# A two-layer hybrid decoder step on one core: another opening, the root table loaded earlier, the output stored in four pieces

## The chip, the core and the metric

The kernel runs on one core of a Trainium2 chip. The core has TensorE (PE; its weight loads, PEld, overlap its products), VectorE (DVE), ScalarE (ACT), GpSimd (POOL) and the queue of SyncE (SP); transfers are issued from SP and POOL and run on 16 shared DMA engines. Time is the device time of one execution in microseconds (us); lower is better. Everything is float32 unless said otherwise.

## What is computed

One inference step of two layers over 256 prompt tokens and 8 sequences of 4 new tokens each, T = 288 columns in all, held as 8 tiles of 128 features. Per layer:

```
xn = rms_norm(x, norm_w)            # x * rsqrt(mean(x*x) + eps) * w
p  = xn @ w_in                      # 35 tiles of 128 output columns
A  = sparse attention over a paged cache (indexer, top-k) * silu(gate)
C  = dilated window attention, 3 groups              * silu(gate)
B  = SSD recurrence (conv, scan, gated rms_norm over groups of 192)
x  = x + concat(A, C, B) @ w_out    # 8 tiles
```

After the second layer `y = rms_norm(x, final_norm_w)` is stored, beside updated caches and states.

## The kernel before, in words

The work is written out by hand, one instruction stream per engine, with a semaphore for every hand-over. Nothing is planned by a scheduler: each engine does its list in order.

**The norm.** For N = 0 (start), 1 (between the layers) and 2 (the end), ACT squares the 8 tiles of x (`square`, L656, into the two buffers `squares`, which lie in tile `cacc`). The sum over the features is a product with a matrix of ones on PE into bank 2. Then ACT takes the square root (`root`, L661) and DVE the reciprocal, which gives `rstd` (L1512). For N = 1 and 2, the first square goes to `tmp`, DVE adds squares 1 to 5 onto it (L2136), and PE sums only three tiles: `tmp` (`sum_added`) and squares 6 and 7 (`sum_squares`). For N = 0, PE sums all eight squares, one product each, before anything else it does, and square k waits until PE has used square k - 2.

**The start.** SP issues the two halves of x (576 KB each), then the parameters `prm` (51 KB), weight tile 0 (512 KB), the page table, weight tiles 1 and 2, constants, and more. DVE multiplies each tile of x by the norm weight (`weighted`, L1517) into `xn`. PE then does `proj(0)`, `proj(1)`, `proj(2)`: 8 products each of a 128x128 weight tile with 128x288 columns. Their results are multiplied by `rstd` afterwards. From `proj(3)` on (`LATE_ROOT`), DVE has multiplied `xn` itself by `rstd` (L1754). When `proj(i)` is complete, SP loads weight tile i + 4, and SP and POOL load the first eight of the `kv` buffers, one or two per projection.

**The page stage.** After `proj(7)` come 16 page pairs, each of whose 16 products read two `kv` buffers that hold records of 8 cache pages (`in_kk`). A ring of 8 buffers is refilled as PE uses them; every second pair is followed by a projection.

**The rest of a layer.** Projections alternate with the indexer's top-k search, the recurrence, window attention and value pages. In it is the norm over groups of 192 features of the SSD result (three tiles of 128): group norm sums `gn0` in bank 2 (tile 0 and the first half of tile 1) and `gn2` in bank 7 (the second half of tile 1 and tile 2), L1426 to L1431, each a product with all or 64 rows of `ones`. At the end `output` (8 tiles) is added into x by DVE (L2130).

**The end.** The final norm's 8 tiles (L2143) are stored by SP in two pieces of 4 tiles (576 KB, L497), each when its tiles are ready.

In the listing, `mm` is one product (two PE records and two weight loads, since float32 takes two passes), `tt_` and `ts_` are DVE operations, and `S[...]` are semaphores.

## Time and profile before

| | us |
|---|---|
| median of 3 runs | 614.76 (609.92, 614.76, 616.73) |
| the profiled execution | 617.67 |
| its span, first to last instruction | 615.9 |
| PE busy / PEld busy | 593.1 / 418.7 |
| DVE / POOL / ACT busy | 357.6 / 276.1 / 169.7 |
| transferred | 198.37 MB, mean 322 GB/s |

The profile is of one execution. A timeline row gives the start and the length of a group of like instructions; "[0.46 <-ACT cacc L656]" says that the engine had been idle for 0.46 us and that ACT's write to `cacc` ended it. A matmul's length contains its latency, so how fast PE goes is read from the distance between starts, best from those of its weight loads. The granted clock is 1.00 at 2.4 GHz and 0.50 at 1.2 GHz.

### The profile page before, as it was taken

The numbers are of one execution on the slowest core, as the hardware profiler recorded it, in microseconds if no ns is written. First come the engines' busy times: TensorE is split into PE (matmuls) and PEld (weight loads), VectorE is DVE, ScalarE is ACT, GpSimd is POOL, SyncE is SP. The second block draws the span as 40 slices with busy tenths as digits, with TensorE's granted clock in tenths as the row PEclk, the third lists the DMA queues.
The fourth block names the chain that finished last, engine by engine and source line by source line (L and its number), as shares of the span: only waits on it lengthen the run. The fifth ranks groups of instructions, "written<-read, shape, count | busy, mean of one in ns | idle before, by whom it ended". The sixth has DMA issues, their size and how long they took to land.

```text
span 615.9 us, 13773 instructions
## 1 busy us (share of the span) xinstructions
PE 593.1 (96%) x4850; PEld 418.7 (68%) x4850; DVE 357.6 (58%) x1068; ACT 169.7 (28%) x429; POOL 276.1 (45%) x476
## 2 busy tenths in 40 slices
PE   5999999999999999999999999999999999999993
PEld 3776655677777766667777665557777786667772
DVE  3674655667657934843348563747776794484224
ACT  4013532223221503441111252323321250354011
POOL 0415642477721594444210275327774159544420
PEclk9999999998889989999999999999998998999998
DMA  8798999999997899999954699999999879979996
GB/s 321 253 328 297 368 367 386 406 377 363 357 378 233 244 341 295 299 314 407 352 179 136 212 368 368 373 414 391 383 356 383 299 246 348 291 225 305 363 326 230
DMA packets 80821, 198.37 MB, mean 322 GB/s; under 512 B 12049, under 2 KB 44978, under 8 KB 80242
## 3 DMA queue, kind: packets, MB, share of 16 engines
q0 software_dynamic: 28768, 102.22, 47.0%
q1 hardware_dynamic: 51986, 95.28, 44.2%
q8 instruction: 39, 0.64, 0.4%
q14 instruction: 28, 0.23, 0.1%
HBM read 189.30 MB, written 52.00 MB: 392 GB/s over the span
## 4 chain that ended last, share of the span: by engine, by line
PE 85%; DMA 9%; issue 2%; SPq 1%; DVE 1%; POOL 1%; ACT 1%; POOLq 0%; ACTq 0%; DVEq 0%
PE bank L898 82%; DMA kv<-in_kk 7%; PE bank L948 3%; DMA kv<-in_vv 1%; SPq L423 1%; DMA x<-in_x 1%; POOL kv L423 1%; DVE xn L2143 1%; DVE rstd L1512 0%; POOL xwb L547 0%; ACT cacc L656 0%; ACT L656 0%; SPq L419 0%; POOLq L419 0%; POOLq L423 0%
## 5 line engine op out<-in xcount | busy, mean ns | idle before, releaser
L898 PE MATMUL bank<-xn,w 128*128 128x288 f32 x1120 | 297.6, 421 | 0.0
L898 PEld LDWEIGHTS bank<-xn,w 128*128 128x128 f32 x1120 | 210.5, 194 | 68.7 <-issue 12.5
L423 POOL DMA_DIRECT2D kv<-in_kk x128 | 69.0, 539 | 121.7 <-issue 68.1
L423 POOL DMA_DIRECT2D kv<-in_vv x128 | 68.9, 541 | 53.5 <-PE bank L898 41.9
L689 ACT ACTIVATE pt<-bank 128x288 f32<-128x288 f32 x48 | 19.7, 411 | 231.7 <-PE bank L898 231.6
L898 PE MATMUL bank<-pt,kv 128*128 128x288 f32 x256 | 62.4, 406 | 0.0
L898 PEld LDWEIGHTS bank<-pt,kv 128*128 128x128 f32 x256 | 48.5, 190 | 13.4
L1587 DVE TENSOR_SCALAR_CACHE_REDUCE hit<-sc,tb 128x516 bf16<-128x516 f32 x62 | 46.5, 750 | 2.2
L898 PE MATMUL bank<-kv,pt 128*32 128x256 f32 x512 | 33.8, 385 | 2.5 <-DMA kv<-in_vv 2.5
L524 POOL DMA_DIRECT2D out_keep<-in_buf x48 | 24.5, 510 | 25.4 <-PE bank L898 23.6
L898 PE MATMUL bank<-kv,qz 128*32 128x256 f32 x512 | 34.3, 385 | 0.0
L2130 DVE TENSOR_TENSOR x<-x,bank 128x288 f32<-128x288 f32 x16 | 7.3, 454 | 45.4 <-PE bank L898 45.3
L1560 DVE COPY tails<-cin 128x3 f32<-128x3 f32 x14 | 5.9, 424 | 42.3 <-ACT cin L687 40.1
L413 POOL DMA_DIRECT2D kv<-in_dil x16 | 9.0, 561 | 44.5 <-PE bank L898 44.5
L1598 DVE TENSOR_SCALAR tb<-bank 128x1 int32<-128x1 f32 x62 | 9.6, 154 | 32.2 <-PE bank L898 31.6
L898 PE MATMUL bank<-kv,shared 128*32 128x128 f32 x768 | 25.8, 291 | 0.0
L898 PE MATMUL bank<-pt 64*128 64x128 f32 (+3 forms) x168 | 25.8, 332 | 0.0
L898 PEld LDWEIGHTS bank<-pt 64*128 64x128 f32 (+2 forms) x168 | 17.7, 183 | 11.0 <-issue 10.3
L898 PEld LDWEIGHTS bank<-kv,pt 128*32 128x32 f32 x512 | 13.6, 109 | 16.5 <-issue 7.6
L1566 DVE SCALAR_TENSOR_TENSOR cacc<-cin,prm,cacc 128x312 f32<-128x312 f32 x42 | 22.8, 544 | 1.5
L898 PEld LDWEIGHTS bank<-kv,shared 128*32 128x32 f32 x768 | 22.1, 116 | 0.6 <-issue 0.5
L656 ACT ACTIVATE cacc<-x 128x288 f32<-128x288 f32 x22 | 9.6, 442 | 46.2 <-DVE x L2130 42.4
(251 smaller groups left out, 818.6 us busy)
## 6 DMA issues: line engine op xcount, KB each, us to landing
w<-in_w SPq DMA_DIRECT2D x70, 512.0 KB, 7.3
out_keep<-in_buf POOLq DMA_DIRECT2D x16, 1984.0 KB, 14.3
kv<-in_kk SPq DMA_DIRECT2D x128, 160.0 KB, 8.1
kv<-in_kk POOLq DMA_DIRECT2D x128, 160.0 KB, 5.8
kv<-in_vv SPq DMA_DIRECT2D x128, 128.0 KB, 4.2
kv<-in_vv POOLq DMA_DIRECT2D x128, 128.0 KB, 4.3
kv<-in_dil SPq DMA_DIRECT2D x16, 576.0 KB, 9.7
kv<-in_dil POOLq DMA_DIRECT2D x16, 576.0 KB, 8.1
```

The source lines that it names most:

```text
L413: engine.dma_start(kv[:, s, 0:9 * P], a["dil"][layer, item]).then_inc(S[f"kv_in{s}"], 16)
L423: engine.dma_start(kv[:, s, r * rec:(r + 1) * rec], a["kk" if what == "page" else "vv"][bass.ds(page + layer * N_POOL, 1)].rearrange("o p ...
L524: pool.dma_start(dst[:, cut:].rearrange("o (r k) -> (o r) k", r=16), src[:, cut:].rearrange("o (r k) -> (o r) k", r=16)).then_inc(S["copie ...
L656: act.activation(tmp[:, :] if N and k == 0 else squares[:, k % 2, 0:T], x[:, k, :], ACT.Square).then_inc(S["sq_ready"], 1)
L689: act.activation(ptile(i), src[:, 0:T], fn).then_inc(use, 1)
L898: return pe.matmul(out, lhsT, rhs, start=start, stop=stop, skip_group_check=True, **k)
L948: return pe.transpose(out, in_, ident(n))
L1566: stt(out=o, in0=cin[:, n % 2, j:j + COUT], scalar=prmc(L, "cw", 4 * n + j), in1=o, op0=ALU.mult, op1=ALU.add).then_inc(S["cin_used"] if j ...
L1587: ts_(hit[:, :], sc[:, :], old.bitcast(F32), 0.0, ALU.is_ge, ALU.add, accum_out=cnt[:, 0:1]).then_inc(S["cnt_ready"], 1)
L1598: ts_(tb[:, 2:3], src[:, 0:1], float(TOPK_S), float(bit), ALU.is_lt, ALU.mult).then_inc(drained(f"count{n}"), 1)
L2130: tt_(x[:, m, :], x[:, m, :], src[:, 0:T], ALU.add).then_inc(drained(f"out{m}"), 1)
L2143: dve.scalar_tensor_tensor(out=xn[:, k, :], in0=x[:, k, :], scalar=fnw[:, k:k + 1], in1=rstd[:, :], op0=ALU.mult, op1=ALU.mult).then_inc(S ...
```

## The change

The opening's sums take the form that the other two norms have: the first square goes to `tmp`, DVE adds five squares onto it between its multiplications, and PE has three products of sums left, which now stand behind `proj(0)`. Ahead of `proj(0)`, PE does twelve products of `ones` with itself (`WARM`) into bank 7, whose result nobody reads. SP issues `prm` first, then the first half of x, weight tile 0, and the second half of x. ACT takes the root of one column of `eps` (`root_table`) ahead of the squares of each norm, so that the table load goes there. The two half-row products of the group norm come behind both full ones. y is stored in four pieces of 2 tiles (288 KB).

```diff
--- before.py
+++ after.py
@@ -52,6 +52,7 @@
 WSLOTS = 4
 DT_ROW, WI_ROW = 0, 32
 PSLOTS = 32
+WARM = 12
 SLOTS = {QI: 0, KI: 4, QA: 12, XBC: 5, QC: 14, KC: 17, KA: 20, VA: 22, VC: 24, GA: 27, GC: 29, ZZ: 0}
 
 
@@ -199,7 +200,7 @@
 
 
 PER = {
-    "rstd_ready": 1, "sq_ready": 8, "sq_added": 5, "sq_used": 7, ...
+    "rstd_ready": 1, "sq_ready": 8, "sq_added": 5, ...
     "qs_ready": 1, "relu_used": 1, "prelu_used": 8, "cnt_ready": NCOUNT + 1, "cin_used": 7, "tanhed": 7, "conved": 7,
     "qz_ready": 1, "qcz_zero": 1, "so_sel": 1, "qcz_ready": 6, "qcbd_ready": 6, "mask_ready": 1, "sexp_in": 1, "sexp": 1, "px_ready": 1,
     "pexp_in": 2, "pexp": 2, "pprob": 2, "dexp_in": 2, "dexp": 2, "dprob": 2,
@@ -226,6 +227,7 @@
         ones = sb("ones", [P, P])
         eps = sb("eps", [P, 1])
         fnw = sb("fnw", [P, KT])
+        rooted = sb("rooted", [P, 1])
         ptab = sb("ptab", [1, NPTAB], I32)
 
         x = sb("x", [P, KT, T])
@@ -444,10 +446,10 @@
                 sync.dma_start(w[:, n % WSLOTS, :, :].rearrange("p k n -> p (k n)"),
                                a["w"][n // NTILE, n % NTILE]).then_inc(S[f"w_in{n % WSLOTS}"], 16)
 
-            for n in range(2):
-                sync.dma_start(x[:, 4 * n:4 * n + 4, :], a["x"][:, 4 * n:4 * n + 4, :]).then_inc(S[f"x_in{n}"], 16)
             sync.dma_start(prm[:, :, :], a["prm"]).then_inc(S["prm_in"], 16)
+            sync.dma_start(x[:, 0:4, :], a["x"][:, 0:4, :]).then_inc(S["x_in0"], 16)
             load_w(0, 0)
+            sync.dma_start(x[:, 4:8, :], a["x"][:, 4:8, :]).then_inc(S["x_in1"], 16)
             sync.dma_start(ptab[:, :], a["ptab"]).then_inc(S["ptab_in"], 16)
             load_w(0, 1)
             load_w(0, 2)
@@ -492,10 +494,10 @@
                     consumed(*RING[lo:hi])
                     next_w(28 + i)
                 consumed(*RING[80:])
-            for n in range(2):
-                sync.wait_ge(S["y_normed"], 4 * n + 4)
-                sync.dma_start(a["y"][:, 4 * n:4 * n + 4, :], xn[:, 4 * n:4 * n + 4, :]).then_inc(S["y_out"], 16)
-            sync.wait_ge(S["y_out"], 32)
+            for n in range(4):
+                sync.wait_ge(S["y_normed"], 2 * n + 2)
+                sync.dma_start(a["y"][:, 2 * n:2 * n + 2, :], xn[:, 2 * n:2 * n + 2, :]).then_inc(S["y_out"], 16)
+            sync.wait_ge(S["y_out"], 64)
 
 
         @block.gpsimd
@@ -649,17 +651,20 @@
                     act.wait_ge(S[f"x_in{k // 4}"], 16)
                 else:
                     act.wait_ge(drained(f"out{k}"), nth(N - 1, f"out{k}"))
-                if N == 0 and k >= 2:
-                    act.wait_ge(S["sq_used"], k - 1)
-                if N and k >= 3:
-                    act.wait_ge(S["sq_added"], nth(N - 1, "sq_added", k - 2))
-                act.activation(tmp[:, :] if N and k == 0 else squares[:, k % 2, 0:T], x[:, k, :], ACT.Square).then_inc(S["sq_ready"], 1)
+                if k >= 3:
+                    act.wait_ge(S["sq_added"], nth(N, "sq_added", k - 2))
+                act.activation(tmp[:, :] if k == 0 else squares[:, k % 2, 0:T], x[:, k, :], ACT.Square).then_inc(S["sq_ready"], 1)
 
             def root(N):
 
                 act.wait_ge(S["ssum_ready"], nth(N, "ssum_ready", 1))
                 act.activation(rstd[:, :], bank[2][:, 0:T], ACT.Sqrt, bias=eps[:, :], scale=1.0 / D_MODEL).then_inc(S["root_ready"], 1)
 
+            def root_table():
+
+                act.activation(rooted[:, :], eps[:, :], ACT.Sqrt)
+
+            root_table()
             for k in range(KT):
                 square(0, k)
             root(0)
@@ -883,6 +888,7 @@
                 prompt_turned(0)
                 prompt_turned(1)
                 evac(34)
+                root_table()
                 for k in range(KT):
                     square(L + 1, k)
                 root(L + 1)
@@ -900,19 +906,17 @@
             def sum_squares(N, k):
 
                 pe.wait_ge(S["sq_ready"], nth(N, "sq_ready", k + 1))
-                ins = mm(bank[2][:, 0:T], ones[:, :], squares[:, k % 2, 0:T], start=(N == 0 and k == 0), stop=(k == KT - 1))
+                ins = mm(bank[2][:, 0:T], ones[:, :], squares[:, k % 2, 0:T], start=False, stop=(k == KT - 1))
                 if k == KT - 1:
                     ins.then_inc(S["ssum_ready"], 1)
-                elif N == 0:
-                    ins.then_inc(S["sq_used"], 1)
 
             def sum_added(N):
 
-                pe.wait_ge(S["sq_added"], nth(N - 1, "sq_added", 5))
+                pe.wait_ge(S["sq_added"], nth(N, "sq_added", 5))
                 mm(bank[2][:, 0:T], ones[:, :], tmp[:, :], start=True, stop=False)
 
-            for k in range(KT):
-                sum_squares(0, k)
+            for n in range(WARM):
+                mm(bank[7][:, 0:P], ones[:, :], ones[:, :])
             for L in range(DEPTH):
                 def bit_count(n):
 
@@ -1143,7 +1147,9 @@
 
                 for i in range(6):
                     proj(i)
-                    if L and i == 0:
+                    if L == 0 and i == 0:
+                        sum_added(0)
+                    if i == 0:
                         sum_squares(L, KT - 2)
                         sum_squares(L, KT - 1)
                 if L == 0:
@@ -1423,12 +1429,11 @@
                 ins.then_inc(filled("dot"), 1)
                 value_groups(10, 12)
                 pe.wait_ge(S["ysq"], nth(L, "ysq", 3))
-                for t, parts in ((0, ((0, slice(0, P)), (1, half(0)))), (2, ((1, half(1)), (2, slice(0, P))))):
+                for t in (0, 2):
                     pe.wait_ge(drained(f"gn{t}"), before(L, f"gn{t}"))
-                    out = bank_of(f"gn{t}")
-                    for n, (k, rows) in enumerate(parts):
-                        ins = mm(out[:, 0:T], ones[rows, :], xwf[rows, k * T:(k + 1) * T], start=(n == 0), stop=(n == 1))
-                    ins.then_inc(filled(f"gn{t}"), 1)
+                    mm(bank_of(f"gn{t}")[:, 0:T], ones[:, :], xwf[:, t * T:(t + 1) * T], start=True, stop=False)
+                for t, rows in ((0, half(0)), (2, half(1))):
+                    mm(bank_of(f"gn{t}")[:, 0:T], ones[rows, :], xwf[rows, T:2 * T], start=False).then_inc(filled(f"gn{t}"), 1)
                 value_groups(12, 16)
                 dilated_turn(0)
                 proj(31)
@@ -1512,6 +1517,12 @@
                 dve.reciprocal(rstd[:, :], rstd[:, :]).then_inc(S["rstd_ready"], 1)
                 dve.wait_ge(S["rstd_ready"], nth(N, "rstd_ready", 1))
 
+            def square_added(N, k):
+
+                dve.wait_ge(S["sq_ready"], nth(N, "sq_ready", k + 1))
+                dve.tensor_tensor(tmp[:, :], tmp[:, :], squares[:, k % 2, 0:T], ALU.add).then_inc(S["sq_added"], 1)
+                dve.wait_ge(S["sq_added"], nth(N, "sq_added", k))
+
             def weighted(N, k):
 
                 dve.tensor_scalar(xn[:, k, :], x[:, k, :], prmc(N, "nw", k), None, ALU.mult).then_inc(S["xw_ready"], 1)
@@ -1739,6 +1750,8 @@
                         if k % 4 == 0:
                             dve.wait_ge(S[f"x_in{k // 4}"], 16)
                         weighted(0, k)
+                        if k in (3, 4, 5, 6, 7):
+                            square_added(0, k - 2)
                     o = PR["cw"][0]
                     ts_(prm[:, :, o:o + 35], prm[:, :, o:o + 35], 0.5, None, ALU.mult).then_inc(chain.next(), 1)
                     dve.wait_ge(S["dve_chain"], chain.n)
@@ -2132,9 +2145,7 @@
                         dve.wait_ge(drained(f"out{m}"), nth(L, f"out{m}"))
                         weighted(L + 1, m)
                     if 2 <= m <= 6:
-                        dve.wait_ge(S["sq_ready"], nth(L + 1, "sq_ready", m))
-                        tt_(tmp[:, :], tmp[:, :], squares[:, (m - 1) % 2, 0:T], ALU.add).then_inc(S["sq_added"], 1)
-                        dve.wait_ge(S["sq_added"], nth(L, "sq_added", m - 1))
+                        square_added(L + 1, m - 1)
                 dve.wait_ge(S["dve_chain"], chain.n)
                 dve.sem_clear(S["dve_chain"])
                 dve.wait_ge(drained(f"out{KT - 1}"), nth(L, f"out{KT - 1}"))
```

PE's first instructions before the change; `xn,w` is a projection, `cacc,ones` a sum of squares:

```order
L898 MATMUL bank<-cacc,ones 128x288 [waits sq_ready,ones_set]
L898 MATMUL bank<-cacc,ones 128x288 [waits sq_ready] x7
L898 MATMUL bank<-xn,w 128x288 [waits xw_ready,drained0,w_in0]
L898 MATMUL bank<-xn,w 128x288 [waits xw_ready] x7
L898 MATMUL bank<-xn,w 128x288 [waits drained1,w_in1]
```

and in the changed kernel:

```order
L904 MATMUL bank<-ones 128x128 [waits ones_set]
L904 MATMUL bank<-ones 128x128 x11
L904 MATMUL bank<-xn,w 128x288 [waits xw_ready,drained0,w_in0]
L904 MATMUL bank<-xn,w 128x288 [waits xw_ready] x7
L904 MATMUL bank<-tmp,ones 128x288 [waits sq_added]
L904 MATMUL bank<-cacc,ones 128x288 [waits sq_ready] x2
L904 MATMUL bank<-xn,w 128x288 [waits drained1,w_in1]
```

The eight sums ahead of the first projection have become three behind it, and the twelve products wait only for `ones`.

DVE's opening before, behind its memsets; L1517 is `weighted`, L1512 the reciprocal:

```order
L1517 TENSOR_SCALAR xn<-x,prm 128x288 [waits x_in0,prm_in,zeroed]
L1517 TENSOR_SCALAR xn<-x,prm 128x288 x3
L1517 TENSOR_SCALAR xn<-x,prm 128x288 [waits x_in1]
L1517 TENSOR_SCALAR xn<-x,prm 128x288 x3
L1743 TENSOR_SCALAR prm<-prm 128x2x35
L1512 RECIPROCAL rstd<-rstd 128x288 [waits root_ready,dve_chain]
```

and in the changed kernel, where L1528 is `weighted`, L1523 the addition of a square:

```order
L1528 TENSOR_SCALAR xn<-x,prm 128x288 [waits x_in0,prm_in,zeroed]
L1528 TENSOR_SCALAR xn<-x,prm 128x288 x3
L1523 TENSOR_TENSOR tmp<-tmp,cacc 128x288 [waits sq_ready]
L1528 TENSOR_SCALAR xn<-x,prm 128x288 [waits x_in1,sq_added]
L1523 TENSOR_TENSOR tmp<-tmp,cacc 128x288 [waits sq_ready]
L1528 TENSOR_SCALAR xn<-x,prm 128x288 [waits sq_added]
...
L1523 TENSOR_TENSOR tmp<-tmp,cacc 128x288 [waits sq_ready]
L1756 TENSOR_SCALAR prm<-prm 128x2x35 [waits sq_added]
L1517 RECIPROCAL rstd<-rstd 128x288 [waits root_ready,dve_chain]
```

Five additions stand between the multiplications, each behind a square of ACT's; the first comes before the wait for the second half of x, the second behind the first multiplication of that half.

PE at the group norm of a layer, before (`xw,ones`):

```order
L898 MATMUL bank4<-kv,pt 32x256 x3
L898 MATMUL bank2<-xw,ones 128x288 [waits drained2,ysq]
L898 MATMUL bank2<-xw,ones 128x288
L898 MATMUL bank7<-xw,ones 128x288 [waits drained7]
L898 MATMUL bank7<-xw,ones 128x288
L898 MATMUL bank4<-kv,pt 32x256 [waits kv_in4]
```

and in the changed kernel:

```order
L904 MATMUL bank4<-kv,pt 32x256 x3
L904 MATMUL bank2<-xw,ones 128x288 [waits drained2,ysq]
L904 MATMUL bank7<-xw,ones 128x288 [waits drained7]
L904 MATMUL bank2<-xw,ones 128x288
L904 MATMUL bank7<-xw,ones 128x288
L904 MATMUL bank4<-kv,pt 32x256 [waits kv_in4]
```

The order was full, half, half, full, and is full, full, half, half.

## Rows read from the trace of the kernel before

**Rows 1.** The page: busy time (us, share of the span, instructions) and the chain's shares.
```profile
PE 593.1 (96%) x4850; PEld 418.7 (68%) x4850; DVE 357.6 (58%) x1068; ACT 169.7 (28%) x429; POOL 276.1 (45%) x476
...
PE 85%; DMA 9%; issue 2%; SPq 1%; DVE 1%; POOL 1%; ACT 1%; POOLq 0%; ACTq 0%; DVEq 0%
```

**Rows 2.** Timeline 0:30: start us, length us, engine, line, what [idle before <-releaser].
```profile
1.02 0.17 DVE L1503 MEMSET ones<- 128x128 f32 x1
...
4.77 1.28 ACT L656 ACT_TABLE_LOAD   x1 [4.77 <-DMA x<-in_x]
...
6.47 2.32 DVE L1517 TENSOR_SCALAR xn<-x,prm 128x288 f32<-128x288 f32 x8 [3.38 <-DMA prm<-in_prm]
...
6.65 7.40 PE L898 MATMUL bank<-cacc,ones 128*128 128x288 f32 x16 [6.65 <-ACT cacc L656]
...
9.50 0.50 PEld L898 LDWEIGHTS bank<-cacc,ones 128*128 128x128 f32 x2 [0.46 <-ACT cacc L656]
...
13.65 16.44 PEld L898 LDWEIGHTS bank<-xn,w 128*128 128x128 f32 x68
...
18.02 0.33 SPq L444 DMA_DIRECT2D w<-in_w  x1
```

**Rows 3.** Transfers of tile in_x: issues (ns min/median/max, first and last start), time to landing.
```profile
L448 SPq DMA_DIRECT2D x<-in_x x2: 394/408/421, 0.9 to 1.3; - x2
...
DMA to landing us min/median/max: 3.8/4.3/4.9
```

**Rows 4.** Windows: us, busy us per engine (records), granted clock, DMA share, GB/s.
```profile
15.30:18.70 3.40, 3.40 (x15) 2.66 (x14) 2.27 (x2) 0.00 (x0) 0.00 (x0) 1.00 0.02 6
...
42.00:50.00 8.00, 7.96 (x103) 5.04 (x102) 6.02 (x23) 2.74 (x8) 0.95 (x2) 1.00 0.55 180
```

**Rows 5.** Timeline 270:345, the end of layer 0 and the start of layer 1.
```profile
287.09 0.44 ACT L656 ACTIVATE tmp<-x 128x288 f32<-128x288 f32 x1 [6.98 <-DVE x L2130]
...
291.94 0.45 DVE L1517 TENSOR_SCALAR xn<-x,prm 128x288 f32<-128x288 f32 x1
292.32 0.44 DVE L2136 TENSOR_TENSOR tmp<-tmp,cacc 128x288 f32<-128x288 f32 x1
...
310.90 3.83 PEld L898 LDWEIGHTS bank<-xn,w 128*128 128x128 f32 x16
...
314.78 0.92 PEld L898 LDWEIGHTS bank<-cacc,ones 128*128 128x128 f32 x4
```

**Rows 6.** The chain of waits: start us, us, what; around the first page products.
```profile
46.16 16.45 PE bank L898 x200
67.43 13.89 DMA kv<-in_kk
```

**Rows 7.** Timeline 237:242.5 of PEld: weight loads of the group norm, layer 0.
```profile
239.37 0.30 PEld L898 LDWEIGHTS bank<-xw,ones 128*128 128x128 f32 x2 [0.52 <-issue]
240.06 0.30 PEld L898 LDWEIGHTS bank<-xw,ones 64*128 64x128 f32 x4 [0.39 <-issue]
240.74 0.30 PEld L898 LDWEIGHTS bank<-xw,ones 128*128 128x128 f32 x2 [0.39 <-issue]
241.43 1.02 PEld L898 LDWEIGHTS bank<-kv,pt 128*32 128x32 f32 x24 [0.39 <-issue]
```

**Rows 8.** Timeline 590:617, then the transfers of tile out_y (issues, time to landing).
```profile
604.53 1.52 PE L898 MATMUL bank<-cacc,ones 128*128 128x288 f32 x4
...
605.27 1.28 ACT L661 ACT_TABLE_LOAD   x1
...
606.56 0.50 ACT L661 ACTIVATE rstd<-bank,eps 128x288 f32<-128x288 f32 x1
...
L497 SPq DMA_DIRECT2D out_y<-xn x2: 343/344/344, 611.0 to 612.7; - x2
...
DMA to landing us min/median/max: 2.8/2.8/2.8
```

**Rows 9.** Windows of 8 us; this one in the recurrence stage of layer 0.
```profile
166.00:174.00 8.00, 8.00 (x59) 5.46 (x49) 3.98 (x15) 1.25 (x5) 3.14 (x7) 0.79 0.99 364
```

More of the change, by code:

```diff
@@ L201 @@
 PER = {
-    "rstd_ready": 1, "sq_ready": 8, "sq_added": 5, "sq_used": 7, "y_normed": 8, "xw_ready": 8, "xn_free": 7, "xn_ready": 8, "roped": 15, "shuffled": 7, "ssum_ready": 1, "root_ready": 1,
+    "rstd_ready": 1, "sq_ready": 8, "sq_added": 5, "y_normed": 8, "xw_ready": 8, "xn_free": 7, "xn_ready": 8, "roped": 15, "shuffled": 7, "ssum_ready": 1, "root_ready": 1,
     "qs_ready": 1, "relu_used": 1, "prelu_used": 8, "cnt_ready": NCOUNT + 1, "cin_used": 7, "tanhed": 7, "conved": 7,
```

## The prediction

> **What bounds the kernel now.** I read the page first: PE is busy 96% of the span and holds 85% of the chain that ended last, DMA 9% [rows 1]. So a microsecond counts where PE stands idle or works for nothing that must come first, and at the end, where only ACT, DVE and the last store are left. I then read the timeline of the start, the boundary between the layers, the group norm and the end.
>
> At the start PE does nothing until ACT's first square, at 6.65 us; ACT's own table load stands between x landing (4.77) and that square, and DVE waits until 6.47 for `prm` [rows 2]. The eight sums take PE from 6.65 to the first load of a projection's weights at 13.65. The row at 9.50 shows one of them: 0.46 idle and 0.50 of loading, so 0.96 us each. At the boundary a product of the same shape takes 3.87 / 8 = 0.48 us (from 310.90 to 314.78) [rows 5]. Twice the time is the 1.2 GHz level: PE had done nothing before 6.65 and stayed low for most of the 7.0 us. From 13.65 PE runs without a gap, and the row ends only at 30.09.
>
> **The start, step by step.** The second half of x is what the new order waits for last. Before, the halves were issued at 0.9 and 1.3 and landed 3.8 and 4.9 us later, at 4.7 and 6.2 [rows 3]: 1.5 us for 0.59 MB. Now the first half has `prm` ahead of it: one issue (0.4) and its 0.05 MB (0.1), so about 5.2. Weight tile 0 (0.52 MB) takes 1.3, to 6.5, and the second half another 1.5, to 8.0. From there: DVE multiplies tile 4 and adds a square, and so on to tile 7. At the boundary a multiplication starts 0.38 before the addition behind it, which takes 0.44 [rows 5]; with the hand-over to itself I take 0.86 a pair. Tile 7's multiplication starts at 8.0 + 3 x 0.86 = 10.6 and ends at 11.0. ACT keeps up (a square is 0.44 [rows 5]). PE has done tiles 0 to 3 by then; it does the product of tile 7 (0.48) and three sums (1.44, all inputs there by 11.9), and starts `proj(1)` at 12.9. Before, it started at 13.65 + 3.88 = 17.5. **Gain 4.6 us.**
>
> This supposes 2.4 GHz by 11.0. The twelve products of ones can start at 1.2 (the memset of `ones` ends at 1.19) [rows 2]; at 0.50 of loading each, as in the row at 9.50, they last until 7.2, and then `proj(0)` has its weights. PE will have worked about as long as it did before its products shortened. They cost nothing themselves: weight tile 0 lands at 6.5, so at most 0.7 of them is in the way, and PE waits for DVE afterwards. Were the level still low, the last four products would cost 1.9 more and the next ones as well. Bounds of this term: 2.0 (low level, late x) to 5.3 (second half of x at 7.3, from less delay by `prm`). I take 4.6, because each of its steps has a row of its own shape.
>
> **Does it travel?** The first page loads and weight tile 4 are issued when `proj(0)` is complete: 18.02 before [rows 2], 11.6 now. The DMA engines idled from 15.3 to 18.7 (share 0.02) [rows 4], so they gain those 3.4 us, and what is queued then (constants, weight tile 3) is needed only by `proj(3)` at 20.7. From 42 to 50 their share is 0.55: the eight `kv` buffers were full before the first page product at 46.16 [rows 6]. PE will now be there at 41.5. The page stage itself is held by DMA (the chain has one wait of 13.89 us [rows 6]), but each refill waits for PE's use of a buffer, so it starts and ends earlier by as much. DVE's chain of `rstd`, projections 0 to 2 and `xn` then has the same order as at the boundary. `proj(3)` gets its first `xn` at about 17.9, before it asks at 20.7. I carry the 4.6 in full.
>
> **The group norm.** Weight loads of full, half and half, full tiles start at 239.37, 240.06 and 240.74, and the next work at 241.43 [rows 7]: 0.69, 0.68, 0.69. A full product alone is 0.48, so a change of tile height costs 0.2; the four half loads lie in one 0.30, which is why the pair costs no more than one. They were neighbours already. With both full ones together one change of height goes: 0.2 per layer, **0.4 us** in all, PE being on the path. Bounds 0 to 0.6.
>
> **The root table.** The table load at the end starts at 605.27, behind the last square, and the root at 606.56, whereas PE's last sum ends at 604.53 + 1.52 = 606.05 [rows 8]. Without the load the root starts 0.03 after the sum: **0.5 us**. Its new place costs nothing: ACT is idle 6.98 us before the first square of a layer's end [rows 5], against 1.28 for the load. At the boundary the root waited for PE anyhow. At the start the load runs while x is on its way; that is in the 4.6.
>
> The Trainium skill's page "ScalarE: Activation LUTs" (What ACT_TABLE_LOAD costs) adds a drain of about 1.38 us to the 1.28 us load at every switch. By that the root would have started at 607.9, and moving the load would be worth 1.9 instead of 0.5. The row at 606.56 leaves no room for it.
>
> **The store.** The two pieces were issued at 611.0 and 612.7 and took 2.8 each [rows 8], so the last landed at 615.5. Four pieces are issued as their tiles come, 0.9 apart against 0.34 per issue, the last again at 612.7. It has half the bytes: 0.29 MB, which at 1.5 us per 0.59 MB [rows 3] is 0.7 less. **0.7 us**; bounds 0 (the time is latency) and 0.8.
>
> The page "DMA: Bandwidth & Descriptors" (Specifications) of the Trainium skill says that rows under 512 B do not reach line rate, and `prm` has rows of 408 B. That speaks against putting it in front; the page has no price for it, and no run here shows one apart.
>
> **Sum.** 4.6 + 0.4 + 0.5 + 0.7 = 6.2 us. The profiled execution would go from 617.67 to 611.5; it is 2.9 above the median shown. From the median, 614.76 - 6.2 = **608.6**.
>
> **The rivals.**
> - *The start is later than that* (chance 0.15). The second half of x lands at 9 rather than 8, or the twelve products do not bring the clock and PE's last four products are long. For it: x has two more transfers ahead, and the clock before rose only late in the sums. Against: the landings in rows 3 leave little room. Either costs 1.0 to 1.9: 610.1.
> - *The page stage swallows the start* (0.11). If the DMA engines, not PE's place, fix when the stage ends, only 1.6 is left: 613.2. For it: the 13.89 us wait [rows 6]. Against: the idle shares of 0.02 and 0.55 [rows 4].
> - *A table load costs more than its row* (0.03). If ACT stands still behind a load for as long again (1.28), the end gives that much more: 607.3. Against: the root at 606.56 starts 0.01 behind the load's end [rows 8]. The Trainium skill's drain (What ACT_TABLE_LOAD costs, in "ScalarE: Activation LUTs") would be this case.
> - *Slower than before* (0.09). In the recurrence, behind stretches of small products, PE falls from 2.4 to 1.2 GHz for a while: over 8 us the mean granted clock is 0.79 [rows 9], so one fall costs 0.21 x 8 = 1.7 us. The page's digits show a few such places. All stages now lie 4.6 us earlier, and the start has a PE that works and pauses in turn. Four further falls eat the 6.2 (6.2 / 1.7 = 3.6); five give 617.1. For it: the runs before differ by 6.8 us, which is four falls. Against: the stages hold the same instructions, so that falls should come as often as before.
>
> **How the numbers follow.** The forecast has 0.62; its own range is 604.5 to 612.5, the scatter of runs mostly. About 1% (6.1 us) is what a measurement of this kernel can tell from no change, and 608.6 lies on that bound. So half of the 0.62 counts as faster, with that of the table load and some of the scatter of the others: 0.42. Slower by over 1% (620.9) takes eight falls or an accident that I don't see: 0.05. Within 1%: 0.53. The range of 603.8 to 613.8 takes in the late start and the swallowed start and leaves out the slower case and the ends of the scatter.
>
> **What would show it.** Right: `proj(1)`'s first weight load near 12.9; no gap in PE from there to the pages; the first page product near 41.5; the 13.89 us wait no longer; weight loads of the group norm over 1.86 instead of 2.06; no table load behind the last square and the root right behind the sum; the last piece of y landing in 2.1. Wrong: weight loads 0.25 us apart after 8 us, DVE's fifth multiplication after 9, a PE gap at `proj(3)`, or DMA waits in the page stage that grow by what the start gained.

## The result and the profile after

The changed kernel took 605.11 us (median of 16 executions, 600.72 to 611.51), the kernel before 613.08 beside it (16 executions, 609.86 to 617.76). The ratio is 0.985 [0.983, 0.988]: 1.5% faster, where the forecast said 608.6 and gave just over half of its chance to "within 1%". The ratio and its interval are of the fast executions alone: twelve of the sixteen, with a median of 604.0, while the four others showed a clock of 0.975 to 0.979 and took 610.0 to 611.5. The profiled execution took 606.05, its span 604.4; before, 617.67 and 615.9.

**The page**, busy time and the chain's shares:
```profile
PE 588.7 (97%) x4864; PEld 418.4 (69%) x4864; DVE 360.0 (60%) x1073; ACT 168.6 (28%) x431; POOL 275.9 (46%) x476
...
PE 91%; issue 2%; DMA 2%; POOL 2%; DVE 1%; POOLq 1%; ACT 0%; SPq 0%; DVEq 0%
```
Against [rows 1] PE works 4.4 us less and the span is 11.5 shorter. The chain's DMA share is 2% instead of 9%. Nothing in the forecast touches that share, so I looked there after the start.

**The start**, timeline 0:24 (the same columns as in [rows 2]), and the transfers of x as in [rows 3]:
```profile
0.88 1.28 ACT L665 ACT_TABLE_LOAD   x1 [0.88 <-PEq L2308]
...
1.24 5.19 PEld L904 LDWEIGHTS bank<-ones 128*128 128x128 f32 x24 [1.24 <-DVE ones L1508]
...
7.40 1.75 PEld L904 LDWEIGHTS bank<-xn,w 128*128 128x128 f32 x8 [0.97 <-DMA w<-in_w]
...
8.89 0.37 DVE L1528 TENSOR_SCALAR xn<-x,prm 128x288 f32<-128x288 f32 x1 [1.07 <-DMA x<-in_x]
...
9.32 0.33 PEld L904 LDWEIGHTS bank<-xn,w 128*128 128x128 f32 x2 [0.16 <-DVE xn L1528]
...
12.00 0.41 PEld L904 LDWEIGHTS bank<-tmp,ones 128*128 128x128 f32 x2
...
12.47 0.92 PEld L904 LDWEIGHTS bank<-cacc,ones 128*128 128x128 f32 x4
...
13.44 10.62 PEld L904 LDWEIGHTS bank<-xn,w 128*128 128x128 f32 x44
```
```profile
L450 SPq DMA_DIRECT2D x<-in_x x1: 421/421/421, 1.3 to 1.3; - x1
L452 SPq DMA_DIRECT2D x<-in_x x1: 431/431/431, 2.3 to 2.3; - x1
...
DMA to landing us min/median/max: 4.8/5.7/6.5
```
The row of 13.44 begins with `proj(1)`'s first weight load, which was at 17.53. The second half of x was issued at 2.27 and landed 6.5 later, at 8.8. The clock had come up: the pair of loads at 9.32 takes 0.33 for one product, and the sums at 12.47 take 0.92 for two, as at the boundary.

**The page stages**, the chain of waits (start us, us, what):
```profile
42.08 69.39 PE bank L904 x709
111.47 0.80 PE bank L952 x6
...
334.61 69.39 PE bank L904 x709
404.00 0.80 PE bank L952 x6
```
All 709 products of the stage are one piece: PE waits for no page. The same chain before, from the row of 46.16 that [rows 6] has:
```profile
92.79 13.22 DMA kv<-in_kk
106.05 11.66 PE bank L898 x77
117.72 0.80 PE bank L948 x6
...
344.38 43.44 PE bank L898 x496
390.00 13.35 DMA kv<-in_kk
...
415.06 0.80 PE bank L948 x6
```
The stage ran from 46.16 to 117.72, 71.56 us, with two DMA rows in the chain (67.43 and 92.79); in layer 1 it took 70.68 (344.38 to 415.06), with one. Now it is 69.39 in both layers.

**The group norm**, PEld 228:233, answers to [rows 7]:
```profile
229.80 0.78 PEld L904 LDWEIGHTS bank<-xw,ones 128*128 128x128 f32 x4 [0.51 <-issue]
230.96 0.30 PEld L904 LDWEIGHTS bank<-xw,ones 64*128 64x128 f32 x4 [0.39 <-issue]
231.65 1.45 PEld L904 LDWEIGHTS bank<-kv,pt 128*32 128x32 f32 x32 [0.38 <-issue]
```
1.85 us from the first load to the next work, before 2.06.

**The end**, timeline 591:604.4 and the store, answers to [rows 8]:
```profile
592.61 1.52 PE L904 MATMUL bank<-cacc,ones 128*128 128x288 f32 x4
...
594.16 0.50 ACT L661 ACTIVATE rstd<-bank,eps 128x288 f32<-128x288 f32 x1 [0.84 <-PE bank L904]
...
596.75 3.52 DVE L2154 SCALAR_TENSOR_TENSOR xn<-x,fnw,rstd 128x288 f32<-128x288 f32 x8
```
```profile
L499 SPq DMA_DIRECT2D out_y<-xn x4: 332/338/344, 597.7 to 600.3; - x4
...
DMA to landing us min/median/max: 2.8/2.8/3.6
```
The root starts 0.03 behind the sum (592.61 + 1.52). But the last quarter of y lands 3.6 after its issue; before, a half took 2.8. DVE ends at 600.27, the span 4.1 later; before, 3.2. The first three quarters took 2.8 each in this trace; in every other trace with four pieces they took 2.1. Why all four are 0.5 to 0.7 longer in this one is open.

**The clock.** The window that fell in [rows 9] has its like here:
```profile
166.00:174.00 8.00, 8.00 (x82) 6.15 (x82) 5.13 (x18) 0.57 (x4) 3.64 (x5) 0.79 1.02 399
```
Such falls come and go between executions of one kernel. Each execution's record has its mean granted clock (0.975 to 0.991 for the changed kernel). I fitted the times of all 274 executions of this case with one level per kernel and one common slope: 0.65 us for each 0.001 of mean clock, with 1.0 us left over. This compares kernels **at equal clock**, here 0.985. The kernel before then takes 613.4 and the changed one 604.9: 8.5 +- 0.5 less. The experiments below are given both ways, the ratio first. The fit is a calculation of mine: it takes the slope as the same for all and counts a clock that a kernel itself lowers as scatter. By it the six sets of executions of the kernel before, taken beside the experiments on four chips, lie between 613.2 and 614.1.

### The profile page after: what moved, and what is told of

Same layout as the page of the kernel before. It is cut to its first block, busy times and chain, and to the rows that moved or that the text cites. A ratio compares the mean times of both kernels' runs of the same rounds, so it can differ in the third digit from the quotient of the medians.

```text
span 604.4 us, 13808 instructions
## 1 busy us (share of the span) xinstructions
PE 588.7 (97%) x4864; PEld 418.4 (69%) x4864; DVE 360.0 (60%) x1073; ACT 168.6 (28%) x431; POOL 275.9 (46%) x476
## 4 chain that ended last, share of the span: by engine, by line
PE 91%; issue 2%; DMA 2%; POOL 2%; DVE 1%; POOLq 1%; ACT 0%; SPq 0%; DVEq 0%
PE bank L904 88%; PE bank L952 3%; POOL kv L425 1%; DMA w<-in_w 1%; DMA kv<-in_vv 1%; POOL xwb L549 1%; DVE xn L2154 1%; DVE rstd L1517 0%; POOLq L421 0%; POOLq L425 0%; DVE hit L1598 0%; DVE xw L1846 0%; ACT rstd L661 0%; DVE x L2143 0%; ACT cacc L656 0%
## 5 line engine op out<-in xcount | busy, mean ns | idle before, releaser
L904 PEld LDWEIGHTS bank<-xn,w 128*128 128x128 f32 x1120 | 208.1, 193 | 68.6 <-issue 11.9
```

What stands on the lines that cost most here:

```text
L904: return pe.matmul(out, lhsT, rhs, start=start, stop=stop, skip_group_check=True, **k)
```

## The experiments

### The two kernels again, and the opening alone


> The kernel before, unchanged, with a trace of its own from the same chip as the three runs beside it. Open: the page stages (first page product to the recurrence) took 71.6 and 70.7 us in the trace of before and 69.4 twice in the trace of after, while the DMA engines moved about 370 GB/s before and 404 GB/s after at the same busy share. Theory A (the rate belongs to the chip or the run): here the rate is near that of the changed kernel beside it, both stages take 69.4 to 70, and the ratio is 1.00. Theory B (the change of place makes the transfers faster): 370 GB/s and 70.7 to 71.6 us again, while the changed kernel on the same chip has 404 and 69.4.

> The changed kernel, unchanged, on the same chip. Ratio 0.985 (0.983 to 0.988). First weight load of the second projection at 13.4 us; last piece of y lands 3.6 us after its issue if that is a property of four pieces, 2.1 to 2.8 if it was an accident of one trace. Theory A: the page stages are as long as in the unchanged kernel's trace beside it, and the ratio is explained by 4.1 us of start, 0.4 of group norm, 0.5 of root and the clock's falls; theory B: they are 1.3 to 2.2 us shorter.

Measured: before again 1.001 [0.998, 1.004]; changed again 0.987 [0.983, 0.991], 8.7 +- 0.8 less at equal clock. Both traces are from one chip. In e1's the page stages take 71.04 and 71.02 us and the DMA engines move 367 GB/s from 58 to 74; in e2's it is 69.39 twice and 404 GB/s. So the shorter stages belong to the kernel and not to the chip. The two profiles of the kernel before have spans of 615.9 and 608.3. The low clock (one minus the granted clock, summed over windows of 4 us from 26 to 590) took 10.2 us of the one and 3.4 of the other: 6.8 of the 7.6 between them.

The opening alone (the new order of SP, ACT, PE and DVE at the start, with `rooted`; root table of the other norms, group norm and store as before):
```diff
                 evac(34)
-                root_table()
                 for k in range(KT):
...
-            for n in range(4):
-                sync.wait_ge(S["y_normed"], 2 * n + 2)
+            for n in range(2):
+                sync.wait_ge(S["y_normed"], 4 * n + 4)
```


> The opening alone: order of the first transfers, twelve products of ones, five squares added by DVE, three sums behind the first projection, root table at the start. Root table at the other norms, group norm and store as before. Theory A (the start is 4.1 us and nothing multiplies it): 4.1 us, ratio 0.9933. Theory B (the start also shortens the page stages by 1.3 to 2.2 us each): 7 to 8 us, ratio 0.987 to 0.989.

Measured: 0.985 [0.982, 0.988], 7.9 +- 0.8 less at equal clock. So nearly all of the gain is in the opening's edits, yet they bring PE to the first page product only 4.4 us earlier (41.73). They hold something else.

> The changed kernel with y stored in two pieces of four tiles again. If four pieces delay the last landing (3.6 us after its issue against 2.8), this is 0.8 us faster than the changed kernel and the distance from the last operation of DVE to the end of the span falls from 4.1 to 3.3 us. If 3.6 was an accident, it is 0.7 us slower, as I had predicted for the bytes.

Measured (the change with the store in two pieces as before): 0.981 [0.979, 0.984], 8.5 +- 0.8 less at equal clock; the lower ratio comes with a mean clock of 0.9887, the highest of all. Neither of the two expected differences (0.8 less or 0.7 more than the changed kernel) came: four pieces bring nothing over two here, though each piece is half as large.

### Where the page stage's 1.3 to 2.2 us come from
In the changed kernel the DMA engines move more at the same busy share. Windows of core 0, before and after:
```profile
58.00:74.00 16.00, 15.35 (x171) 9.60 (x170) 9.97 (x24) 8.90 (x22) 11.80 (x19) 1.00 1.04 369
```
```profile
58.00:74.00 16.00, 16.00 (x184) 9.71 (x174) 10.98 (x29) 7.81 (x20) 10.23 (x17) 1.00 1.04 403
```
The only edit that reaches these transfers is `rooted`: a tile of 4 bytes per partition, which takes 32. All tiles allocated behind it move by 32 bytes, `kv` from byte 112608 (224 above a multiple of 256) to 112640 (a multiple of 512), `w` from 49376 to 49408 (a multiple of 256).

**e5**: the kernel before with a tile that nothing uses; no instruction differs.
```diff
         fnw = sb("fnw", [P, KT])
+        gap = sb("gap", [P, 8])
```


> The kernel before with one unused buffer of 32 bytes per partition where the changed kernel has the new column `rooted`; no instruction differs. It moves x, xn, the weight slots and the kv buffers by 32 bytes: w starts at 49408 instead of 49376, kv at 112640 instead of 112608 (multiples of 256 instead of 224 above one). Theory A (the address sets the rate of the transfers): about 403 GB/s in the page stages instead of 368, page stages of 69.4 us without DMA waits instead of 70.7 to 71.6, and 4 us in all: ratio 0.992 to 0.995. Theory B (the earlier start sets it): 368 GB/s, waits as before, ratio 1.000.

Measured: 0.996 [0.992, 0.999], 3.6 +- 0.6 less at equal clock. Chain and window:
```profile
46.02 69.39 PE bank L899 x709
115.41 0.80 PE bank L949 x6
```
```profile
58.00:74.00 16.00, 16.00 (x174) 10.18 (x173) 9.98 (x24) 8.75 (x22) 11.83 (x19) 1.00 1.04 403
```
The start is the old one (46.02), the stage the new one (69.39).

**e6**: the change with `rooted` allocated behind the large tiles.
```diff
-        rooted = sb("rooted", [P, 1])
...
         cbs = sb("cbs", [32, 64])
+        rooted = sb("rooted", [P, 1])
```


> The changed kernel with the column `rooted` allocated behind all other buffers, so that x, xn, w and kv have the addresses of the kernel before; instructions as in the changed kernel. Theory A: 368 GB/s and DMA waits in the page stages, ratio 0.991 to 0.994 (start, group norm and root are left, 5 us). Theory B: 403 GB/s, no waits, ratio 0.985 to 0.987.

Measured: 0.996 [0.992, 1.000], 4.3 +- 0.6 less at equal clock. The start is the new one, the stage the old one, 70.81 us with a wait for a page in it:
```profile
41.47 43.44 PE bank L904 x496
86.94 13.63 DMA kv<-in_kk
100.61 11.66 PE bank L904 x77
112.28 0.80 PE bank L952 x6
```
```profile
58.00:74.00 16.00, 16.00 (x176) 9.61 (x175) 10.92 (x30) 7.25 (x18) 9.79 (x18) 1.00 1.05 368
```
e5 and e6 are the two halves of the change: 3.6 + 4.3 = 7.9, against 8.5 +- 0.5 together. By the terms of its trace (start 4.3, group norm 0.4, root 0.5, store -0.3) e6 should give 4.9, which its error of 0.6 just takes in.

**e7**: another shift, 96 bytes, made by allocating `nacs` ahead of `ptab`; `kv` then begins at 112704, a multiple of 64 but 64 above one of 256.
```diff
         fnw = sb("fnw", [P, KT])
+        nacs = sb("nacs", [P, 3, 6])
```


> The kernel before with `nacs` (96 bytes) allocated ahead of the page table, which moves x, xn, w and kv by 96 bytes: kv starts at 112704, a multiple of 64 but 64 above a multiple of 256; w at 49472, likewise. No instruction differs. If a multiple of 64 is enough: 403 GB/s, ratio as with 32 bytes (0.992 to 0.995). If it takes a multiple of 256, as the Trainium skill's page DMA: Bandwidth & Descriptors (How a descriptor splits into AXI transactions) has it for the ends of a transfer: 368 GB/s, DMA waits, ratio 1.000.

Measured: 0.999 [0.994, 1.003], 0.1 +- 0.6 more at equal clock:
```profile
58.00:74.00 16.00, 16.00 (x174) 10.18 (x173) 9.98 (x24) 8.95 (x22) 11.82 (x19) 1.00 1.04 368
```
Neither the shift as such nor 64 bytes help.

**e12**: the change with two store pieces; `xn4` is allocated ahead of `x`, and `st4`, `st4b`, `relun` and `cnt` ahead of `w`, so that `kv` is at 112896, 256 above a multiple of 512.


> The changed kernel with its store in two pieces; some small tiles are allocated ahead of x and ahead of w, so that x and xn too begin at multiples of 256 bytes (they stood 128 above one) and kv moves from a multiple of 512 to 256 above one; the instructions are the same. Theory (what matters for the page records is a multiple of 256): 402 to 405 GB/s and 69.4 us per page stage as with kv at 112640. Rival (it takes a multiple of 512): 370 GB/s, 71 us, and a ratio about 0.5% higher. For x and xn, whose rows are 4608 bytes, one boundary in 19 is saved: at most 0.1 us per half, no measurable gain; ratio 0.980 to 0.982.

Measured: 0.988 [0.984, 0.992], 8.3 +- 0.6 less at equal clock, 69.39 in both layers, and
```profile
58.00:74.00 16.00, 16.00 (x175) 9.36 (x173) 10.93 (x30) 7.01 (x18) 9.80 (x18) 1.00 1.04 404
```
So of the places tried, multiples of 256 are fast and those 64 and 224 above are slow. In the window from 58 to 74 all twelve traces with `kv` at a multiple of 256 have 403 to 405 GB/s and the seven others 367 to 369. Alignment of `x` and `xn` brought nothing more.

No run moves `kv` without `w`, but the packets in this window tell them apart. From the kernel before to e5, the 5120-byte packets into `kv` (POOL's queue) fall from a mean of 222 ns to 197, the 1280-byte packets (SP's queue) from 59.8 to 55.3, and the 4096-byte packets into `w` from 165 to 159. By the packet counts (516, 1750 and 242) over nine tenths of the saved time is in `kv`; this share is an estimate.

The page records are rows of 1280 bytes, five times 256. The Trainium skill's page "DMA: Bandwidth & Descriptors" (How a descriptor splits into AXI transactions) says that a descriptor is split into transactions of 256 bytes and that, when it does not start at a multiple of 256, its first transaction starts at the boundary below it. The page speaks of bytes that are read; here it is the destination that moved. An estimate by that rule, carried over to the destination: 5 transactions become 6 for both offsets, and 40 beats of 32 bytes become 47 at 224 above and 42 at 64 above. The traces agree with the first in that both offsets cost the same. The size does not come out of it: it would be 20% for packets of 1280 bytes and 5% for those of 5120, and the traces have 8% and 13%, 9% of the rate together. So the effect of the address is shown; by what mechanism it arises is not.

### The start
**e9**: the twelve products of ones left out (store in two pieces).
```diff
-WARM = 12
+WARM = 0
```


> The changed kernel with its store in two pieces, and without the twelve products of ones at the start. Theory (they bring TensorE's clock up ahead of the first tile): PE begins at 1.2 GHz with proj(0) at about 6.3; a product lasts 0.96 there against 0.48, the last products of proj(0) and the three sums are long, and the first page product comes at 43 to 44 instead of 41.3, so the ratio to the kernel before is about 0.985 instead of 0.9814. Rival (what waits for x and DVE hides it): first page product at 41.3 to 41.8, ratio 0.981. For the late landing of y's last piece (3.7 us where the kernel before has 2.8): if the added products are its reason, it falls back to 2.8 here and the time from DVE's last instruction to the end of the span to 3.2; if not, it stays at 3.7 and 4.2.

Measured: 0.995 [0.992, 0.998], 6.4 +- 0.6 less at equal clock than before: 2.1 of e4's 8.5 are gone, and its mean clock, 0.9803, is the lowest of all. PEld at the start:
```profile
6.89 5.79 PEld L904 LDWEIGHTS bank<-xn,w 128*128 128x128 f32 x16 [6.89 <-issue]
12.74 0.43 PEld L904 LDWEIGHTS bank<-tmp,ones 128*128 128x128 f32 x2
13.22 0.92 PEld L904 LDWEIGHTS bank<-cacc,ones 128*128 128x128 f32 x4
```
The eight products of `proj(0)` take 5.79 and come straight behind one another, since PE is now behind DVE; the sums at 12.74 are at full pace. The first page product is at 42.83, against 41.30 in e4: 1.5. What of the lower clock is e9's own doing the fit can't tell.

**e10**: the kernel before with `prm` ahead of both halves of x.
```diff
+            sync.dma_start(prm[:, :, :], a["prm"]).then_inc(S["prm_in"], 16)
             for n in range(2):
                 sync.dma_start(x[:, 4 * n:4 * n + 4, :], a["x"][:, 4 * n:4 * n + 4, :]).then_inc(S[f"x_in{n}"], 16)
-            sync.dma_start(prm[:, :, :], a["prm"]).then_inc(S["prm_in"], 16)
```


> The kernel before with one move: prm is loaded ahead of both halves of x. No other instruction and no address changes. Both halves land 0.3 to 1.0 later, the first page product comes at 46.5 to 47 against 46.16, the page stages stay at 71 us and 370 GB/s, and the ratio to the kernel before is 1.000 to 1.002. If the order of the first transfers is why y's last piece lands late, that landing is 3.7 here instead of 2.8; if the reason lies in the instructions of the engines, it is 2.8.

Measured: 1.002 [0.998, 1.006], 0.9 +- 0.6 more at equal clock; the first page product at 45.88, no later than in the other old openings (45.15 to 46.23); last piece of y in 2.8.

**e11**: the change with two store pieces, x's first half ahead of `prm`.
```diff
-            sync.dma_start(prm[:, :, :], a["prm"]).then_inc(S["prm_in"], 16)
             sync.dma_start(x[:, 0:4, :], a["x"][:, 0:4, :]).then_inc(S["x_in0"], 16)
+            sync.dma_start(prm[:, :, :], a["prm"]).then_inc(S["prm_in"], 16)
```


> The changed kernel with its store in two pieces, and x's first half ahead of prm. If prm in front delays x and with it the start: the first half lands at 4.7 instead of 5.2 to 6.1, and the first page product comes 0.3 to 0.6 earlier than 41.3. If instead the multiplications, which need prm, set the pace: prm lands about 1.0 later than 3.1 and the first page product comes at 41.3 to 42, nothing gained. Ratio 0.980 to 0.983 in both. y's last piece: 2.8 if prm in front is why it lands late, else 3.7.

Measured: 0.990 [0.985, 0.994], 7.7 +- 0.8 less at equal clock; the first half of x landed at 4.7 instead of 5.3 to 6.1, but DVE then waited for `prm` until 4.96, the second half still landed at 8.6, and the first page product came at 41.88. Nothing is gained by it, as the second branch said. `prm` in front delays the first half; it was not what made the second half late.

### The end
**e8**: the kernel before with its store in four pieces.
```diff
-            for n in range(2):
-                sync.wait_ge(S["y_normed"], 4 * n + 4)
+            for n in range(4):
+                sync.wait_ge(S["y_normed"], 2 * n + 2)
```


> The kernel before with y stored in four pieces of two tiles, addresses as before. Last landing after its issue: 2.1 us instead of 2.8, and 2.6 us instead of 3.3 from DVE's last operation to the end of the span (0.7 us, ratio 0.999). If four pieces cost by themselves: 2.8 or more, and no gain. In the traces with shifted buffers the last of two pieces took 3.7 and the last of four 3.1 and 3.6, against 2.8 unshifted.

Measured: 0.999 [0.995, 1.003], 0.3 +- 0.6 less at equal clock. Each piece lands in 2.1, and the span ends 2.5 behind DVE instead of 3.2: the forecast's 0.7, by itself. None of the kernels with the new opening so far has it: there it is 4.1, 3.5 and 3.5 with four pieces (the change's two profiles and e6) and 4.2 with two (e3, e4, e9, e11, e12). e9 rules out the twelve products, e10 and e11 the place of `prm`, e5 and e6 the addresses. What those kernels have in common is 29 packets of instruction fetch on the page instead of 28, one of them in the span's last 3 us, and six more instructions for DVE. (e5 has 29 too, but none in its last 30 us, and lands in 2.8.)

**e14** gives DVE six instructions more on the old opening, and nothing else; **e13** and **e16** give the changed kernel forty and twelve more. This is e16's edit; e14 has 12 in the place of 24, e13 has 80.
```diff
                     dve.wait_ge(S["prm_in"], 16)
                     for k in range(KT):
+                        if k == 0:
+                            for _ in range(24):
+                                dve.wait_ge(S["prm_in"], 16)
```


> The kernel before with the store in four pieces (which landed in 2.1 each) and with twelve waits for prm ahead of DVE's first wait for x: six more instructions for DVE, as many as the change adds, and no other work. Theory (fetch of DVE's code): 29 instruction packets instead of 28, one of them in the last 3 us, the last piece lands in 3.0 to 3.6, and DVE's end to the end of the span is 3.5 instead of 2.5. Rival (the opening's order, ACT or PE): 28 packets, last piece in 2.1, 2.5.

Measured: 614.59 us, one execution. DMA queues in the last 4 us, and the landing:
```profile
q14 instruction: 1, 0.01, 0.5%
```
```profile
DMA to landing us min/median/max: 2.1/2.1/3.1
```
The span ends 3.5 behind DVE's last instruction. Six instructions on DVE, and the last piece is 1.0 late. This is one execution against one of e8; but the rule holds in all 19 traces. The nine with a fetch in their last 2.4 us end 0.9 to 1.0 later behind DVE than the others with as many pieces (the first profile of the change 1.5), and the ten without one end 2.5 or 3.2 behind DVE.

> The changed kernel with 80 waits for prm, long landed, ahead of DVE's first wait for x: forty more instructions for DVE and no other work. Theory (the last piece of y lands late because an instruction fetch of DVE's code, pushed there by six more instructions, uses one of the DMA engines at that moment): the fetch moves some forty instructions ahead of the end, away from the store; the last piece lands in 2.1 us, the time from DVE's last instruction to the end of the span falls from 3.5 to 4.1 to 2.5, and the ratio to the kernel before from 0.985 or 0.987 to about 0.984. Rival (it is something else in the new opening): landing 2.8 to 3.6, no fetch near it needed, ratio as the changed kernel. The waits lie in the time in which DVE waits for x; if they last over 2.3 us, the start is later by the rest.

Measured: 0.983 [0.979, 0.987], 8.9 +- 0.8 less at equal clock; the fetch is between 60 and 50 us ahead of the end; all four pieces land in 2.1, and the span ends 2.6 behind DVE. DVE's forty instructions lasted until 6.78 (3.69 of issue), longer than its wait for x, and the first page product was at 41.58.

> The changed kernel with 24 waits for prm (twelve instructions) instead of e13's 80, ahead of DVE's first wait for x. At 0.09 us each they take 1.1 us, between prm at 3.1 and x at 5.4 or later, so the start is the changed kernel's: DVE's fifth multiplication at 8.0 to 8.9, first page product at 41.2 to 42.1. The fetch of DVE's code moves ahead of the store (twelve instructions ahead of the end lie in the last multiplications), so the last piece lands in 2.1 and DVE's end to the end of the span is 2.5. Ratio about 0.983. Rival (twelve are too few, the fetch meets one of the earlier pieces): that piece lands in 3.1, the last in 2.1, and the end is the same 2.5.

Measured: 0.985 [0.979, 0.990], 9.1 +- 0.8 less at equal clock, the most of all. The fetch is 8 to 10 us ahead of the end, before the first piece of y; the span ends 2.6 behind DVE, and the store:
```profile
DMA to landing us min/median/max: 2.1/2.1/2.1
```

### Weight tile 0 behind x
**e15** and **e17** are e13 and e16 with both halves of x ahead of weight tile 0.
```diff
-            load_w(0, 0)
             sync.dma_start(x[:, 4:8, :], a["x"][:, 4:8, :]).then_inc(S["x_in1"], 16)
+            load_w(0, 0)
```


> e13 with both halves of x ahead of weight tile 0. Theory (the start is held by x's second half, which waits behind weight tile 0): the second half lands at 6.2 to 6.5 instead of 8.0 to 8.8, weight tile 0 at 7.5 to 8; DVE has tile 7 by 9.5, PE's proj(0) runs from 7.8 to 11.7 without a pause, and proj(1)'s first weight load comes at about 13.1 to 13.4, the first page product at 41.0 to 41.5: 0 to 0.8 earlier. Rival (weight tile 0 now comes last and holds PE for 1.5 longer while the clock falls behind the twelve products): first page product at 42 to 44. Ratio 0.982 to 0.985 in the first case, 0.985 to 0.988 in the second.

> e16 with both halves of x ahead of weight tile 0. Theory (the start is held by x's second half behind weight tile 0): DVE's fifth multiplication at 6.8 to 7.5 instead of 8.0 to 8.9, tile 7 done by 10, but PE's proj(0) starts only at 8.0 as in e15 and needs 3.7 without a pause: proj(1)'s first weight load at 13.1, first page product at 41.7. Then weight tile 0 and x's second half are worth the same, and the start is bound by the bytes that must land. Rival (weight tile 0 lands by 7): proj(0) ends by 11, proj(1) at 12.3, first page product at 41.0.

Measured: 0.990 [0.986, 0.993] and 0.989 [0.986, 0.992], each above its partner in the same comparison (0.983 and 0.985); at equal clock 0.8 and 0.7 behind them, which is within the errors. First page product 41.83 and 43.76, partners 41.58 and 41.75. In e15 DVE was held by its forty instructions, so it is e17 that tells. x is earlier there (DVE's fifth multiplication at 7.27 instead of 8.56), weight tile 0 later, and PE stands for 2.06:
```profile
1.24 4.93 PEld L904 LDWEIGHTS bank<-ones 128*128 128x128 f32 x24 [1.24 <-DVE ones L1508]
8.23 5.38 PEld L904 LDWEIGHTS bank<-xn,w 128*128 128x128 f32 x16 [2.06 <-DMA w<-in_w]
13.67 0.43 PEld L904 LDWEIGHTS bank<-tmp,ones 128*128 128x128 f32 x2
```
```profile
8.00:16.00 8.00, 7.77 (x25) 5.84 (x26) 2.42 (x8) 2.21 (x5) 0.51 (x1) 0.79 1.00 378
```
`proj(0)` took 5.38 where e15, behind an idle stretch of 1.56, took 3.69. The granted clock of 0.79 over the 8 us says why: a stretch at 1.2 GHz. It came in one of the two profiles of this order, so it is not shown to be a property of it. But neither branch is below e16: weight tile 0 or x, one of them lands last.

## Why the forecast was wrong

**The step that failed** is in "Does it travel?": that the page stage "starts and ends earlier by as much". This takes the stage's length as unchanged, and the sum has no term for it: `rooted` counts only as an operand of ACT, not as 32 bytes in front of every large tile. The step also read the chain short: it has three rows of DMA into `kv`, of 13.89, 13.22 and 13.35 us, and not the one of 13.89. The stage became 2.2 and 1.3 us shorter in the two layers (71.56 and 70.68 to 69.39), 3.5 in the profiles; e5 puts it at 3.6 +- 0.6 without any instruction changed. The rival that the page stage swallows the start went the wrong way too: the DMA waits did fix part of the stage's length, but at 368 GB/s, and the change took them away.

Term by term, forecast and measured:

| term | forecast | measured |
|---|---|---|
| start | 4.6 | 4.1 in the first pair of profiles; 4.3 as the mean of six old openings (45.82) and seven new (41.56) |
| page stages | 0 | 3.5 (profiles), 3.6 +- 0.6 (e5) |
| group norm | 0.4 | 0.2 per layer, 0.4 |
| root table | 0.5 | 0.5: the root is 0.03 behind the sum |
| store | 0.7 | -0.3 to -0.9: 3.5 and 4.1 behind DVE instead of 3.2 |
| sum | 6.2 | 7.6 by the first pair of profiles (with 4.1 and -0.9), 8.4 with 4.3 and -0.3; 8.5 +- 0.5 at equal clock |

The two profiles differ by 11.5; the low clock took 10.2 us of the one and 5.1 of the other. Half of the distance from 608.6 to 605.11 is the starting point: 614.76 was the median of three, 613.08 that of sixteen. The other half, 1.8, is about the 3.5 of the page stages less what the start and the store fell short by: two misses that partly cancel, which is luck and no merit of the sum.

**The start** was right in its mechanism; one landing was late: x's second half at 8.8 instead of 8.0 (8.1 in the change's second profile), the fifth multiplication at 8.89. From there the forecast was 0.3 too long: a pair of multiplication and addition takes 0.77, not 0.86, three times over. The clock was up when it was needed, as supposed. The products do what the text gave them: without them the start is 1.5 later. Of the late-start rival, x came nearly as late as it said (9); its price of 1.0 was 0.5, and its other half, a low clock for the last products, did not occur.

**The group norm and the root** came out as costed. No drain behind a table load shows: the load at the start ends at 2.16 and `rooted` is written at 2.17.

**The store** was right by itself (e8) and wrong in company. The forecast costed DVE's five additions by their time alone. That DVE's code is fetched in packets, and that six more instructions move one of these fetches into the last store, was not in it. The Trainium skill's page "Runtime: NRT & Kernel Launch" (Instruction fetch mechanics) calls the cost of crossing to the next block of code mostly hidden. No run here prices a fetch inside the kernel. At the end, where nothing but the store is left, it is 1.0 us (e8 against e14: 2.1 and 3.1). Why one packet of 8 KB costs as much as that is open; in e4, whose bulk ends at 602.0, only single packets are left until 603.0, so it looks as if one DMA engine lags, but no run tests that.

**Slower by clock falls** (0.09): the changed kernel's clock was hardly lower than before (mean 0.9836 over 16 executions against 0.9844 over 108; by the slope that is 0.5 us).

## What to carry to other kernels

Before costing a diff, ask what each new tile does to the addresses behind it, and where those tiles are the target of DMAs, try a multiple of 256 bytes, the fast one of the places tried here; a gap of 32 unused bytes was worth 3.6 us. When the end of a kernel is a short store, look for an instruction fetch in its last microseconds, and count the instructions of the engine that runs last. And where the clock scatters, compare executions at equal clock: a change of 0.3 to 0.5% can be read that way when the medians can't tell it.

The best version is the change with DVE's fetch moved off the store (e16: 0.985 [0.979, 0.990], 604.3 at equal clock). At equal clock it is 0.6 below the change itself, which the errors (0.8 and 0.5) don't separate; only the store's landing shows it.

## What the runs showed that was not expected

- The rate of the DMAs in the page stage depends on the address of their destination: 403 to 405 GB/s with `kv` at multiples of 256, 367 to 369 at 64 and 224 above, at the same busy share (1.04 to 1.05).
- One instruction fetch during the last store delays its landing by 0.9 to 1.0 us (2.1 to 3.1 for a quarter, 2.8 to 3.7 for a half).
- The clock makes most of the scatter of this kernel: 0.65 us per 0.001 of mean granted clock over 274 executions, with 1.0 us left.
- The granted clock does not show the low level of the opening: it reads 1.00 from 8 to 16 us in e9, where eight products take 5.79 us of loading instead of 3.7. There the level is read from the durations. A later fall, like that in e17 (0.79 over the same 8 us), does show.
- A wait that is already met costs DVE time as well: forty instructions of two waits each took 3.69 us, 0.09 each.
